# A second queue for half of the expert weights: w_up's odd expert issued from GpSimd, the rest from the sync engine

## The chip, the cores and the metric

One core of a Trainium2 chip. The metric is the device time of one execution of the whole kernel, in microseconds. All tensors are float32, batch 1, 256 tokens.

## The reference

A decoder block of width 1024: a mixer (causal pooling beside sliding-window attention, merged by sigmoid gates), then a mixture of experts with 32 experts of which each token uses 4. What costs the time is the second part:

```python
def moe(h, w_router, b_router, w_up, b_up, w_down, b_down):
    logits = (t @ w_router + b_router).astype(jnp.float32)
    top_vals, top_idx = lax.top_k(logits, TOP_K)          # TOP_K = 4
    ...
    for e in range(N_EXPERTS):                            # 32
        act = clamped_swiglu(t @ w_up[e] + b_up[e])       # w_up[e]   1024 x 2048
        out = out + gates[:, e:e + 1] * (act @ w_down[e] + b_down[e])   # w_down[e] 1024 x 1024
    return out.astype(h.dtype).reshape(B, S, D)
```

Every expert is used by some token, so all of w_up (268.4 MB) and w_down (134.2 MB) must come from HBM.

## The kernel before

**Passes and loads.** The experts are worked off in pairs, one pair to a pass, 16 passes: up to 64 tokens of the even expert lie in columns 0 to 63 of the gathered activations, those of the odd expert in columns 64 to 127. A pass takes 12 loads of 2 MiB: 8 of w_up (`UP_LOADS`; four column chunks `j` times two halves of the contraction) and 4 of w_down. Each load fills one slot of `ring`, which has `R` = 10 slots. In a w_up slot the first half holds the even expert's 1 MiB and the second half the odd expert's; each of these comes by a DMA of its own with rows of 2 KiB (`load_expert`, L274 to L284). A w_down load has rows of 8 KiB; the last one of a pass is cut in two with rows of 4 KiB (L289, L292, L293).

**Who issues.** All these DMAs are issued by the sync engine (SP) in one order: `load` 0 to 11 of one pass after the other, the first pass at L317 to L323, the others in a hardware loop of 3 rounds of 5 passes (L335 to L340). Ahead of each load SP waits until TensorE has freed the slot. Since there are 10 slots and 12 loads, `wait_freed` (L325) makes load n of a pass wait for load n + 2 of the pass before (for n below 10), counted in `up_done` and `down_done`. Each slot has a semaphore `full[slot]` that rises by `LANDED` = 32 when the whole slot has landed (16 for each of the two halves of w_up).

**The mixer** is ordered by a list of units (`UNITS`, counted in `unit_done`). Its eleven loads use the same ring; the ones that matter here are the last four (`C_GA`, `C_GA2`, `W_OUT0`, `W_OUT1`), which SP issues after the unit attn1, and after them the first pass's loads, each of which waits for the unit that used its slot last.

**TensorE.** `pe_pass` does a pass: for each chunk a bias matmul (L747) and two loads of matmuls (L768, 8 a load), transposes of the activation (L739), then the four w_down loads (L789, 16 a load), the gather for the next pass (L721), the scatter (L806) and a transpose (L730). `slot_load` (L818) waits for `full` of the slot. VectorE and ScalarE do the activation between them.

**GpSimd** sets some constants at the start, adds up the pooling windows, and issues two DMAs of the mixer (`skew` L390 and `band` L405); after about 46 us it has nothing to do.

Of the kernel before, what the change touches and what calls it, by code (L numbers as in the profile page):

```python
# [15 lines left out]
P = 128  # L16
# [19 lines left out]
PASSES = E // 2  # L36
ROUNDS = SEQ // SLOTS - 1
LISTED = 16
NJ, CH = 4, 512
# [4 lines left out]
R = 10  # L44
SLOT = KD * CH
LANDED = 32

C_U, C_KV, C_Q, C_GP, W_POOL, C_GPA, W_ATTN, C_GA, C_GA2, W_OUT0, W_OUT1 = range(11)
MIXER_LOADS = 11
# [4 lines left out]
LOADS = 12  # L54
UP_LOADS = 2 * NJ
UNROLL = 5
# [15 lines left out]
UNIT = {name: n for n, (name, _) in enumerate(UNITS)}  # L72
# [22 lines left out]
def hybrid_block_kernel(nc, x, norm1_g, w_in, pool_w, pool_scale, w_pool_proj, sinks, w_attn_proj,  # L95
# [4 lines left out]
    w_in_d, w_up_d, w_down_d = w_in[0], w_up[0], w_down[0]  # L100
# [6 lines left out]
    with ExitStack() as ctx:  # L107
        def sb(name, shape, dt=F32):
            return ctx.enter_context(nc.sbuf_tensor(name, shape, dt))

        def sem(name):
            return ctx.enter_context(nc.semaphore(name))

        ring = sb("ring", [P, R, SLOT])
# [94 lines left out]


        full = [sem(f"slot{i}_full") for i in range(R)]
        x_loaded = [sem("x0_loaded"), sem("x1_loaded")]
        vec_loaded, bias_in_loaded = sem("vec_loaded"), sem("bias_in_loaded")
        pw_loaded, sinks_loaded, router_loaded = sem("pw_loaded"), sem("sinks_loaded"), sem("router_loaded")
# [3 lines left out]
        unit_done = sem("unit_done")  # L218
# [12 lines left out]
        up_done = sem("up_done")  # L231
# [4 lines left out]
        down_done = sem("down_done")  # L236
# [11 lines left out]
        def emptied_at(name):  # L248

            n = UNIT[name]  # L250
            by = UNITS[n][1]
            return emptied[by], sum(b == by for _, b in UNITS[:n + 1])
# [10 lines left out]
        @block.sync  # L263
        def _(sp):
            def load_w_in(n, c):
                wide = min(CH, w_in_d.shape[1] - c * CH)
                sp.dma_start(ring[:, n % R, 0:KD * wide].rearrange("p (k n) -> p k n", k=KD),
                             w_in_d[:, c * CH:c * CH + wide].rearrange("(k p) n -> p k n", p=P)).then_inc(full[n % R], LANDED)

            def load_rows(n, src):  # L270
                sp.dma_start(ring[:, n % R, :].rearrange("p (k n) -> p k n", n=D),
                             src.rearrange("(k p) n -> p k n", p=P)).then_inc(full[n % R], LANDED)

            def load_expert(slot, load, expert):  # L274


                dst = ring[:, slot, :]
                if load < UP_LOADS:
                    cols, half = slice(load // 2 * CH, (load // 2 + 1) * CH), slice(load % 2 * CH, (load % 2 + 1) * CH)
                    for e in range(2):  # L280
                        src = w_up_d[bass.ds(expert + e, 1), half, cols].rearrange("e (k p) n -> p (e k) n", p=P)
                        sp.dma_start(dst[:, e * SLOT // 2:(e + 1) * SLOT // 2].rearrange("p (k n) -> p k n", n=CH),  # L282
                                     src).then_inc(full[slot], LANDED // 2)
                else:  # L284
                    m = load - UP_LOADS
                    src = w_down_d[bass.ds(expert, 2), m * CF:(m + 1) * CF, :].rearrange("e (p k) n -> p e (k n)", p=P)
                    dst = dst.rearrange("p (e n) -> p e n", e=2)
                    if load < LOADS - 1:
                        sp.dma_start(dst, src).then_inc(full[slot], LANDED)  # L289
                    else:  # L290

                        sp.dma_start(dst[:, :, 0:D], src[:, :, 0:D]).then_inc(even_landed, 16)  # L292
                        sp.dma_start(dst[:, :, D:2 * D], src[:, :, D:2 * D]).then_inc(full[slot], LANDED)  # L293

            for t in range(TT):
                sp.dma_start(acc[:, t, :], x_d[t]).then_inc(x_loaded[t], 16)

            sp.dma_start(vectors[0:KD, :], norm1_g[0].rearrange("(k p) -> k p", p=P)).then_inc(vec_loaded, 16)
            sp.dma_start(vectors[KD:2 * KD, :], norm2_g[0].rearrange("(k p) -> k p", p=P)).then_inc(vec_loaded, 16)
            sp.dma_start(vectors[2 * KD:2 * KD + KW, :], pool_scale[0].rearrange("(k p) -> k p", p=P)).then_inc(vec_loaded, 16)  # L300
            for n in (C_U, C_KV, C_Q, C_GP):
                load_w_in(n, W_IN_LOAD.index(n))
            load_rows(W_POOL, w_pool_proj[0])
            load_w_in(C_GPA, W_IN_LOAD.index(C_GPA))
            load_rows(W_ATTN, w_attn_proj[0])

            sp.wait_ge(unit_done, UNIT["pool1"] + 1)
            sp.dma_start(bup, b_up_d).then_inc(bup_loaded, 16)

            sp.wait_ge(unit_done, UNIT["attn1"] + 1)  # L310
            load_w_in(C_GA, W_IN_LOAD.index(C_GA))
            load_w_in(C_GA2, W_IN_LOAD.index(C_GA2))
            load_rows(W_OUT0, w_out[0][0:CH, :])
            load_rows(W_OUT1, w_out[0][CH:D, :])

            last_use = ["gate_pool1", "q1", "gate_pool5", "gate_pool7", "gate_attn1", "gate_attn7",
                        "gate_attn5", "gate_attn7", "out3", "out3"]  # L317
            for load in range(LOADS):
                if load < R:
                    sp.wait_ge(unit_done, UNIT[last_use[load]] + 1)  # L320
                else:
                    sp.wait_ge(up_done, load - R + 1)
                load_expert((MIXER_LOADS + load) % R, load, 0)  # L323

            def wait_freed(g, load):  # L325

                back, g0 = load - R, 0
                if back < 0:
                    back, g0 = back + LOADS, -1
                if back < UP_LOADS:  # L330
                    sp.wait_ge(up_done, UP_LOADS * (g + g0) + (back + 1))
                else:
                    sp.wait_ge(down_done, 4 * (g + g0) + (back - UP_LOADS + 1))

            with sp.Fori(0, (PASSES - 1) // UNROLL) as i:  # L335
                for q in range(UNROLL):
                    g = i * UNROLL + (q + 1)
                    for load in range(LOADS):
                        wait_freed(g, load)
                        load_expert((MIXER_LOADS + (q + 1) * LOADS + load) % R, load, g * 2)  # L340


            sp.wait_ge(extra_ready, 1)
            extras = sp.value_load(n_extra[0:1, 0:1], min_val=0, max_val=LISTED)
            with sp.If(extras > 0):
                with sp.Fori(0, extras) as t:
                    pair = sp.value_load(x_pair[0:1, bass.ds(t, 1)], min_val=0, max_val=PASSES - 1)
                    for load in range(LOADS):
                        if load < R:

                            sp.wait_ge(down_done, (t + PASSES) * 4)
                        else:
                            sp.wait_ge(up_done, (t + PASSES) * UP_LOADS + (load - R + 1))
                        load_expert((ALL_LOADS + load - LOADS) % R, load, pair * 2)
            with sp.Else():
                pass

            sp.wait_ge(up_done, (extras + PASSES) * UP_LOADS - (UP_LOADS - 3))
            sp.dma_start(fin_g, final_g.partition_broadcast(P)).then_inc(fin_loaded, 16)
            sp.wait_ge(result_ready, 1)  # L360
            sp.dma_start(out_d[0], result[:, 0, :]).then_inc(stored, 16)
            for n in range(2):
                sp.wait_ge(result_ready, n + 2)
                sp.dma_start(out_d[1][:, n * CH:(n + 1) * CH], result[:, 1, n * CH:(n + 1) * CH]).then_inc(stored, 16)
            sp.wait_ge(stored, 16 * 3)
# [3 lines left out]
        def _(pool):  # L369
# [19 lines left out]
            src = bias_row.unsqueeze(1).broadcast_to([HEADS, P, 3 * WINDOW])  # L389
            nc.gpsimd.dma_start(skew.rearrange("p h i -> h p i"), src).then_inc(skew_written, 16)  # L390

            src = uT
            for step in range(NG):
# [7 lines left out]
                src = dst  # L401
            pool.wait_ge(skew_written, 16)
            pitch = HEADS * 3 * WINDOW
            back = bass.AP(skew.tensor, WINDOW - 1, [[pitch - 1, P], [3 * WINDOW, HEADS], [1, 2 * WINDOW]])
            nc.gpsimd.dma_start(band, back).then_inc(band_loaded, 16)  # L405


        @block.scalar
# [124 lines left out]
        def _(pe):  # L533
# [94 lines left out]
            for i in range(6):  # L628
# [3 lines left out]
                for n in range(4):  # L632
                    if i < 4:
                        src = scores1[:, 2 * i + n // 2, (n % 2) * P:(n % 2 + 1) * P]
                    else:
                        src = scores0[:, 4 * (i - 4) + n, :]
# [179 lines left out]
            def main_slot(i, q):  # L816

                def slot_load(load):  # L818
                    n = MIXER_LOADS + q * LOADS + load
                    pe.wait_ge(full[n % R], i * (LANDED * UNROLL * LOADS // R) + LANDED * (n // R + 1))  # L820
                    return ring[:, n % R, :]
                return slot_load

# [339 lines left out]
```

## Time and profile before

| | |
|---|---|
| median of the runs | 1203.43 us (3 runs, 1203.12 to 1203.86) |
| the profiled execution, span from the first to the last instruction | 1200.5 us |
| TensorE busy | 1105.0 us, 92% |
| VectorE, ScalarE, GpSimd busy | 249.1, 101.6 and 8.9 us |
| moved by DMA | 431.72 MB, 360 GB/s over the span |

The profile shows one execution, whose span is some 3 us shorter than the median of the times, which include what lies around it. The rows further down give busy time by stretch, what the queues moved and what was waited for. The share of a DMA queue can add up to a little over 100%, since the records of packets that follow each other overlap by a few ns.

### The profile page before, as it was taken

The numbers are of one execution on the slowest core, as the hardware profiler recorded it, in microseconds if no ns is written. First come the engines' busy times: TensorE is split into PE (matmuls) and PEld (weight loads), VectorE is DVE, ScalarE is ACT, GpSimd is POOL, SyncE is SP. The second block draws the span as 40 slices with busy tenths as digits, with TensorE's granted clock in tenths as the row PEclk, the third lists the DMA queues.
The fourth block names the chain that finished last, engine by engine and source line by source line (L and its number), as shares of the span: only waits on it lengthen the run. The fifth ranks groups of instructions, "written<-read, shape, count | busy, mean of one in ns | idle before, by whom it ended". The sixth has DMA issues, their size and how long they took to land.

```text
span 1200.5 us, 12804 instructions
## 1 busy us (share of the span) xinstructions
PE 1105.0 (92%) x4941; PEld 498.7 (42%) x4941; DVE 249.1 (21%) x567; ACT 101.6 (8%) x257; POOL 8.9 (1%) x20
## 2 busy tenths in 40 slices
PE   6599998999999999899998989988998989898986
PEld 4488865333434343334342423333333424243332
DVE  2132114121221212122211212111121212121122
ACT  1041012000000000000000000000000000000002
POOL 0200000000000000000000000000000000000000
PEclk9799997999999999899999999998999999999999
DMA  8740995899999999999999999999999999999995
GB/s 240 242 155 2 366 387 196 302 387 407 387 407 387 408 387 407 387 403 390 401 394 397 397 392 403 389 405 386 405 385 407 387 407 385 406 389 401 393 397 208
DMA packets 170500, 431.72 MB, mean 360 GB/s; under 512 B 7479, under 2 KB 9196, under 8 KB 158148
## 3 DMA queue, kind: packets, MB, share of 16 engines
q1 hardware_dynamic: 167368, 427.59, 93.7%
q0 software_dynamic: 976, 2.63, 1.3%
q8 instruction: 47, 0.77, 0.3%
q10 hardware_dynamic: 2092, 0.60, 0.2%
q14 instruction: 17, 0.14, 0.0%
HBM read 428.16 MB, written 2.62 MB: 359 GB/s over the span
## 4 chain that ended last, share of the span: by engine, by line
SPq 64%; PE 24%; DMA 5%; issue 4%; DVE 1%; ACT 0%; DVEq 0%; ACTq 0%
SPq L282 56%; PE bank L564 9%; PE bank L768 6%; SPq L289 5%; DMA ring<-in_w_in 4%; PE bank L789 3%; PE bank L667 2%; DMA ring<-in_w_down 2%; SPq L293 1%; SPq L292 1%; PE bank L721 1%; PE bank L747 1%; PE bank L806 0%; PE bank L684 0%; PE bank L581 0%
## 5 line engine op out<-in xcount | busy, mean ns | idle before, releaser
L768 PE MATMUL bank<-ring,z_buf 128*64 128x512 f32 x2048 | 463.4, 602 | 28.7 <-DMA ring<-in_w_up 28.5
L768 PEld LDWEIGHTS bank<-ring,z_buf 128*64 128x64 f32 x2048 | 141.8, 138 | 345.1 <-issue 279.0
L789 PE MATMUL bank<-ring,m_buf 128*64 128x512 f32 x1024 | 228.3, 596 | 11.5 <-DMA ring<-in_w_down 11.3
L789 PEld LDWEIGHTS bank<-ring,m_buf 128*64 128x64 f32 x1024 | 75.2, 137 | 144.3 <-issue 130.9
L1059 DVE TENSOR_SCALAR swi<-bank 128x256 f32<-128x256 f32 x64 | 27.2, 425 | 390.3 <-PE bank L768 390.3
L564 PE MATMUL bank<-h_buf,ring 128*128 128x256 f32 x400 | 91.9, 386 | 15.4 <-DMA ring<-in_w_in 14.4
L564 PEld LDWEIGHTS bank<-h_buf,ring 128*128 128x128 f32 x400 | 76.9, 194 | 26.9 <-DMA ring<-in_w_in 14.8
L747 PE MATMUL bank<-pw_buf,row_buf 128*128 128x512 f32 x128 | 69.9, 629 | 16.9 <-issue 10.3
L498 ACT ACTIVATE swi<-swi 128x256 f32<-128x256 f32 x64 | 26.7, 416 | 586.2 <-DVE swi L1059 586.2
L721 PEld LDWEIGHTS bank<-u_buf,h_buf 128*128 128x128 f32 x512 | 61.2, 196 | 25.3 <-issue 25.3
L721 PE MATMUL bank<-u_buf,h_buf 128*128 128x128 f32 x512 | 67.4, 286 | 0.1
L806 PE MATMUL bank<-y,u_buf 128*128 128x512 f32 x128 | 61.9, 606 | 1.0
L1070 DVE COPY y<-bank 128x512 f32<-128x512 f32 x16 | 11.1, 692 | 239.7 <-PE bank L789 239.7
L1044 DVE TENSOR_TENSOR z_buf<-bank,small 128x512 f32<-128x512 f32 x32 | 22.1, 692 | 143.0 <-PE bank L721 143.0
L1049 DVE TENSOR_TENSOR acc<-acc,bank 128x512 f32<-128x512 f32 x64 | 43.9, 686 | 11.6 <-PE bank L806 11.1
L739 PEld LDWEIGHTS bank<-ident,m_buf 128*128 128x128 f32 x128 | 20.1, 206 | 52.3 <-issue 52.3
L492 ACT COPY m_buf<-bank 128x256 f32<-128x256 f32 x64 | 23.0, 359 | 142.2 <-PE bank L739 142.2
L806 PEld LDWEIGHTS bank<-y,u_buf 128*128 128x128 f32 x128 | 21.6, 189 | 30.5 <-DVE acc L1049 21.0
L739 PE MATMUL bank<-ident,m_buf 128*128 128x128 f32 x128 | 32.3, 334 | 0.0
L777 PE MATMUL bank<-rt_buf,row_buf 128*128 128x256 f32 x128 | 30.3, 379 | 0.0
L667 PE MATMUL bank<-ring,m_buf 128*128 128x512 f32 x64 | 29.5, 621 | 0.0
L747 PEld LDWEIGHTS bank<-pw_buf,row_buf 128*128 128x128 f32 x128 | 20.2, 199 | 20.8 <-issue 10.8
(163 smaller groups left out, 380.7 us busy)
## 6 DMA issues: line engine op xcount, KB each, us to landing
ring<-in_w_up SPq DMA_DIRECT2D x256, 1024.0 KB
ring<-in_w_down SPq DMA_DIRECT2D x48, 2048.0 KB
ring<-in_w_down SPq DMA_DIRECT2D x32, 1024.0 KB, 23.4
ring<-in_w_in SPq DMA_DIRECT2D x6, 2048.0 KB
ring<-in_w_out SPq DMA_DIRECT2D x2, 2048.0 KB
ring<-in_w_pool_proj SPq DMA_DIRECT2D x1, 2048.0 KB
ring<-in_w_attn_proj SPq DMA_DIRECT2D x1, 2048.0 KB
skew<-y POOLq DMA_DIRECT2D x1, 1536.0 KB, 35.2
```

What stands on the lines that cost most here:

```text
L282: sp.dma_start(dst[:, e * SLOT // 2:(e + 1) * SLOT // 2].rearrange("p (k n) -> p k n", n=CH), src).then_inc(full[slot], LANDED // 2)
L289: sp.dma_start(dst, src).then_inc(full[slot], LANDED)
L564: ins = nc.tensor.matmul(dst, w[:, k, c * P:(c + 1) * P], rhs[:, k, :], start=(k == 0), stop=(k == kn - 1))
L667: ins = nc.tensor.matmul(b[:, :], mixedT[:, k, t * P:(t + 1) * P], w[:, k % 4, n * CH:(n + 1) * CH], start=(k == 0), stop=(k == KD - 1))
L721: ins = nc.tensor.matmul(turn_banks[k // 4][:, (k % 4) * P:(k % 4 + 1) * P], x1r[:, t, k * P:(k + 1) * P], pick[:, t, :], start=(t == 0), ...
L739: ins = nc.tensor.transpose(turn_banks[j % 2][:, c * P:(c + 1) * P], hid[:, j * CF + c:(j + 1) * CF:2], ident[:, :])
L747: nc.tensor.matmul(up_banks[j % 2][:, :], rows[:, j].rearrange("p e s -> p (e s)"), bup, start=True, stop=False, skip_group_check=True)
L768: ins = nc.tensor.matmul(b[e * SLOTS:(e + 1) * SLOTS, :], xgT[:, at, e * SLOTS:(e + 1) * SLOTS], w[:, e, k, :], start=False, stop=(at == K ...
L777: nc.tensor.matmul(down_banks[n][:, c * CF:(c + 1) * CF], rows[:, 2 * n + c].rearrange("p e s -> p (e s)"), bdn, start=(c == 0), stop=Fals ...
L789: ins = nc.tensor.matmul(down_banks[n][e * SLOTS:(e + 1) * SLOTS, :], hidT[:, k, e * SLOTS:(e + 1) * SLOTS], w[:, e, k % 2, n * CH:(n + 1) ...
L806: nc.tensor.matmul(scatter_banks[q % 2][:, :], spreadT[:, t * P:(t + 1) * P], y[:, n * CH:(n + 1) * CH], start=True, stop=True).then_inc(s ...
L1049: nc.vector.tensor_tensor(acc[:, t, n * CH:(n + 1) * CH], acc[:, t, n * CH:(n + 1) * CH], scatter_banks[q % 2][:, :], ALU.add).then_inc(ad ...
```

## The change

A second set of ten semaphores, `odd_full`, is added. In the main passes SP issues only the even expert's half of each w_up slot and lets `full[slot]` rise by 32 with it; w_down stays with SP as it was. The odd expert's half is issued by GpSimd in a loop of its own, with the same conditions on the slot. TensorE waits for both semaphores ahead of a w_up load. The branch for extra passes (more than 64 tokens for an expert) still loads both halves from SP; it isn't taken with these inputs.

```diff
+        odd_full = [sem(f"slot{i}_odd_full") for i in range(R)]
...
-            def load_expert(slot, load, expert):
+            def load_expert(slot, load, expert, experts=(0, 1)):
...
-                    for e in range(2):
+                    for e in experts:
...
-                                     src).then_inc(full[slot], LANDED // 2)
+                                     src).then_inc(full[slot], LANDED // len(experts))
...
-                load_expert((MIXER_LOADS + load) % R, load, 0)
+                load_expert((MIXER_LOADS + load) % R, load, 0, experts=(0,))
...
-                        load_expert((MIXER_LOADS + (q + 1) * LOADS + load) % R, load, g * 2)
+                        load_expert((MIXER_LOADS + (q + 1) * LOADS + load) % R, load, g * 2, experts=(0,))
...
             nc.gpsimd.dma_start(band, back).then_inc(band_loaded, 16)
+
+            def load_odd_expert(slot, load, expert):
+                cols, half = slice(load // 2 * CH, (load // 2 + 1) * CH), slice(load % 2 * CH, (load % 2 + 1) * CH)
+                src = w_up_d[bass.ds(expert + 1, 1), half, cols].rearrange("e (k p) n -> p (e k) n", p=P)
+                nc.gpsimd.dma_start(ring[:, slot, SLOT // 2:SLOT].rearrange("p (k n) -> p k n", n=CH), src).then_inc(odd_full[slot], 16)
+
+            last_use = ["gate_pool1", "q1", "gate_pool5", "gate_pool7", "gate_attn1", "gate_attn7", "gate_attn5", "gate_attn7"]
+            for load in range(UP_LOADS):
+                pool.wait_ge(unit_done, UNIT[last_use[load]] + 1)
+                load_odd_expert((MIXER_LOADS + load) % R, load, 0)
+            with pool.Fori(0, (PASSES - 1) // UNROLL) as i:
+                for q in range(UNROLL):
+                    g = i * UNROLL + (q + 1)
+                    for load in range(UP_LOADS):
+                        back = load - R + LOADS
+                        if back < UP_LOADS:
+                            pool.wait_ge(up_done, UP_LOADS * (g - 1) + (back + 1))
+                        else:
+                            pool.wait_ge(down_done, 4 * (g - 1) + (back - UP_LOADS + 1))
+                        load_odd_expert((MIXER_LOADS + (q + 1) * LOADS + load) % R, load, g * 2)
...
                     pe.wait_ge(full[n % R], i * (LANDED * UNROLL * LOADS // R) + LANDED * (n // R + 1))
+                    if load < UP_LOADS:
+                        nth = sum(m % LOADS < UP_LOADS and (MIXER_LOADS + m) % R == n % R for m in range(q * LOADS + load + 1))
+                        pe.wait_ge(odd_full[n % R], i * (16 * UNROLL * UP_LOADS // R) + 16 * nth)
```

## Rows read from the trace of the kernel before

**Rows 1.** Windows: busy us of each engine, clock, DMA share and rate.
```profile
222.00:1181.00 959.00, 901.69 (x4006) 347.52 (x4002) 189.65 (x417) 59.08 (x157) 0.00 (x0) 0.99 1.04 396
84.00:120.00 36.00, 36.00 (x215) 31.96 (x213) 9.63 (x16) 8.51 (x23) 0.00 (x0) 1.00 0.01 1
267.00:324.00 57.00, 56.48 (x257) 22.02 (x258) 12.32 (x27) 3.78 (x10) 0.00 (x0) 1.00 1.04 398
1068.00:1131.00 63.00, 57.06 (x257) 22.36 (x256) 12.32 (x27) 3.78 (x10) 0.00 (x0) 1.00 1.04 397
```

**Rows 2.** The page: shares of the chain of work that ended last.
```profile
SPq 64%; PE 24%; DMA 5%; issue 4%; DVE 1%; ACT 0%; DVEq 0%; ACTq 0%
```

**Rows 3.** The DMA view, 142 to 160 us, all w_up: packets, MB, share.
```profile
DMA packets 3512, 6.97 MB, mean 387 GB/s; under 512 B 111, under 2 KB 111, under 8 KB 3512
q1 hardware_dynamic: 3512, 6.97, 105.2%
```

**Rows 4.** The DMA view, 1163 to 1173 us, mostly w_down.
```profile
DMA packets 620, 4.21 MB, mean 421 GB/s; under 512 B 32, under 2 KB 32, under 8 KB 131
```

**Rows 5.** SP's instructions in order: start, us, line, count.
```profile
126.18 48.28 SPq L282 DMA_DIRECT2D ring<-in_w_up  x16
194.95 18.35 SPq L289 DMA_DIRECT2D ring<-in_w_down  x3
219.33 0.37 SPq L292 DMA_DIRECT2D ring<-in_w_down  x1
222.94 1.12 SPq L282 DMA_DIRECT2D ring<-in_w_up  x2
```

**Rows 6.** GpSimd's last DMA in order, and the page's row with its landing.
```profile
45.07 0.92 POOL L405 DMA_DIRECT2D ring<-skew  x1 [7.81 <-DMA skew<-y]
ring<-skew POOLq DMA_DIRECT2D x1, 1024.0 KB, 9.8
```

**Rows 7.** The DMA view, 50 to 52 us: both queues at work (q0 is GpSimd's).
```profile
DMA packets 206, 0.72 MB, mean 358 GB/s; under 512 B 1, under 2 KB 1, under 8 KB 206
q0 software_dynamic: 145, 0.59, 82.9%
q1 hardware_dynamic: 61, 0.12, 18.0%
```

**Rows 8.** The DMA view, 128 to 131 us: rows of 1 KiB on SP's queue.
```profile
DMA packets 881, 1.09 MB, mean 362 GB/s; under 512 B 16, under 2 KB 816, under 8 KB 881
```

**Rows 9.** The DMA view, 132 to 140 us: rows of 4 KiB on SP's queue.
```profile
DMA packets 815, 3.27 MB, mean 409 GB/s; under 512 B 16, under 2 KB 16, under 8 KB 815
```

**Rows 10.** TensorE's instructions in order, the mixer's gates.
```profile
125.44 3.62 PE L564 MATMUL bank<-h_buf,ring 128*128 128x256 f32 x16
128.90 1.89 PE L564 MATMUL bank<-z_buf,ring 128*128 128x256 f32 x8
130.62 3.62 PE L564 MATMUL bank<-h_buf,ring 128*128 128x256 f32 x16
```

**Rows 11.** TensorE in order, pass 1: its first up matmuls and last down ones.
```profile
266.90 1.51 PE L768 MATMUL bank<-ring,z_buf 128*64 128x512 f32 x6
310.03 7.09 PE L789 MATMUL bank<-ring,m_buf 128*64 128x512 f32 x32
```

**Rows 12.** TensorE in order, the end of pass 14 and pass 15.
```profile
1117.26 7.09 PE L789 MATMUL bank<-ring,m_buf 128*64 128x512 f32 x32 [0.91 <-DMA ring<-in_w_down]
1131.84 3.65 PE L768 MATMUL bank<-ring,z_buf 128*64 128x512 f32 x16
1181.16 7.09 PE L789 MATMUL bank<-ring,m_buf 128*64 128x512 f32 x32 [0.88 <-DMA ring<-in_w_down]
1188.18 1.98 PE L806 MATMUL bank<-y,u_buf 128*128 128x512 f32 x4
```

**Rows 13.** The chain of waits, the last load of all: start, us.
```profile
1157.72 0.05 issue
...
1157.91 23.11 DMA ring<-in_w_down
```

**Rows 14.** TensorE's waits for w_up, from 222 to 640 us, then to 1181 us: total, times, longest.
```profile
PE bank L768 <- DMA ring<-in_w_up: 0.2, 1, 0.2
...
PE bank L768 <- DMA ring<-in_w_up: 28.5, 25, 2.2
```

## The prediction, made before the change was run

> **What bounds the kernel now.** I read the windows first, because a busy share over the whole span mixes stages. From 222 us to 1181 us, 959 of the span's 1200.5 us, the DMA engines are busy without a break (share 1.04) and move 396 GB/s [rows 1]. TensorE is at work 902 of these 959 us, which looks like a second limit; the single passes settle it. Pass 1, which finds its data in place, takes TensorE 57 us with 56.5 busy; pass 14 takes 63 us with 57.1 busy [rows 1]. The 6 us are waits for data. The chain of waits says the same by the queue: 64% of the span is SP in the act of issuing [rows 2], that is, SP held up by a DMA queue that is full. The rate checks too: in a stretch of w_up alone the engines move 387 GB/s [rows 3], in one that is nearly all w_down 421 GB/s [rows 4]. A pass has 16.78 MB of w_up and 8.39 MB of w_down: 43.4 + 19.9 = 63.3 us, the length of a late pass. So the end is set by bytes over rate, counted from the moment when the stream last stood still, and by what TensorE still has to do once the last byte is there.
>
> That moment is 222.9 us. SP had issued the first pass's w_up by 174.5 us and then waited until 194.95, 219.33 and 222.94 us for slots that TensorE had to free [rows 5].
>
> **Part 1: early loads in the mixer.** GpSimd can issue the first odd halves as soon as their slots are free, ahead of attn1. Between 84 and 120 us the DMA engines do nothing (1 GB/s) [rows 1], so up to 4 MiB can land there for nothing. I cost this at 0. The stream stands still again until 222.9 us for want of slots [rows 5], and the ring holds no more than before; what was fetched earlier only lengthens that pause. There could be a small loss: `C_GA` is issued at 120.3 us and needed by the third gate_attn unit at 130.6 us [rows 10]. If one odd half (1.05 MB, 2.7 us at 387 GB/s) passes it, it lands about 130 instead of 127 us. Nought to 2.7 us; I take 0.
>
> **Part 2: issue time.** SP issues 128 DMAs fewer, but it spends its time waiting for a full queue, not working. 0. TensorE gets 128 more semaphore waits, in the DMA-bound passes inside its idle 6 us; only the last pass could show its eight of them. The short steps of issue in the chain are 0.05 us each [rows 13]; 0 to 0.4 us, I take 0.
>
> **Part 3: the rate of the two queues together.** Nothing here shows a w_up load on GpSimd's queue. The nearest rows are its one load into the ring, with rows of 1 KiB: while it runs, both queues together move 358 GB/s, in packets of 4 KiB (0.59 MB in 145) [rows 7]. SP's queue with rows of the same 1 KiB moves 362 GB/s in a stretch that holds a few larger packets too [rows 8]. For equal rows the two queues are worth the same, so I take 387 GB/s for the odd halves as well: 0. The bounds: if the packing into 4 KiB packets makes 2 KiB rows as good as SP's 4 KiB rows, 409 GB/s [rows 9], the 8.39 MB of odd halves in a pass take 20.5 in place of 21.7 us, 1.2 us by 15 passes, -18 us. If any mixture of the queues runs at 358 GB/s, it covers the odd halves and a fifth as much again of SP's (0.12 beside 0.59 MB [rows 7]), 10.1 MB: 28.2 us instead of 25.8 at the 391 that lies between rows 3 and 4, 2.4 us by 15 passes, +36 us.
>
> **Part 4: the order in which the bytes come.** This is where I see a cost. Before, one queue brings the bytes in just the order in which TensorE wants them. Now GpSimd's queue carries 8 of the 24 half-loads of a pass and its only brake is the freed slot. In the one place where the queues met, q0 moved 0.59 MB and q1 0.12 MB in 2 us [rows 7]: GpSimd's data passes SP's, and also the backlog that stands in SP's queue (the last load waits 23 us between issue and landing [rows 13]). GpSimd's load took 9.8 us from issue to landing, with 1024 rows [rows 6]; one of 512 rows, at most every 7.9 us, can be kept up. So the odd halves will be as far ahead as the ring allows, and the bytes that they take early are missing in SP's stream, on which TensorE then waits. In the middle this costs nothing, as the engines are always busy. At the end it does. The odd halves of pass 15 need slots that pass 14 frees, the last two after its second w_down load. All eight are there, or nearly, when the last w_down load of pass 14 lands. Behind that landing stand only SP's own bytes of pass 15: 8.39 MB at 387 and 8.39 MB at 421 GB/s, 21.7 + 19.9 = 41.6 us. The last byte still lands at 1181.2 us (parts 1 and 3), so pass 14's last w_down lands at 1139.6 instead of 1117.3 us [rows 12]. From there TensorE is the bound: 14.6 us to the first up matmul of pass 15 (1117.26 to 1131.84 [rows 12]), 50.2 us from that to the last down matmul when no data is late (266.90 to 317.12 in pass 1 [rows 11]), 12.3 us from there to the end (1188.25 to 1200.5 [rows 12]). 1139.6 + 14.6 + 50.2 + 12.3 = 1216.7 us, against 1200.5 now. In other words, after the last byte TensorE has 23 us of matmuls left and not 7.
>
> **The sum.** 0 + 0 + 0 + 16.2 us on a span of 1200.5 us. The median is 2.9 us above the profiled span, which I leave: 1219.6 us.
>
> **The Trainium skill on this.** Its page DMA: Bandwidth & Descriptors, section "Issuing engines are not separate DMA queues", says that DMAs from several engines run on the same 16 DMA engines and interleave, so that a second issuer only saves issue time. It speaks against any gain here. By that rule alone the time would stay as it is, at 1203.4 us; it agrees with rows 7 and 8 as to the rate and says nothing of part 4.
>
> **Rivals.** *A, the forecast*: order costs 16 us, the rate is within a per cent or so. *B, faster*: the odd halves go at up to 409 GB/s and the lead is smaller than I think, because with 2 KiB rows the queues share evenly. With no lead at all that is 1203.4 - 18 = 1185.4 us; with the whole lead 1201.6 us. For it speaks the size of q0's packets; against it the 358 GB/s of rows 7. It decides for faster where the rate gains more than the order costs, at 5% on the odd halves with the whole lead. *C, no change*: the engines serve both queues so that the halves of a slot come together, and the rate is the same: 1203.4 us. For it, the same bytes and engines; against it, 145 packets beside 61. *D, much slower*: the mixture is slow, 1219.6 + 36 = 1256 us, or GpSimd can't write its descriptors fast enough. If each of its loads took the 9.8 us of rows 6 with none overlapping, a pass would need 78 us and the kernel some 225 us more. Rows 6 are for twice as many rows, so I hold that for improbable. *E, the change does not do what it says*: the odd halves wait on the same slots so late that GpSimd gains no lead; its time is that of C.
>
> **How the numbers follow.** A 0.73, between 1206 and 1250 us (part 3 taken from a small gain to most of the loss); B 0.12, from 1185 to 1202; C and E 0.09, about 1203; D 0.06, above 1250. A measurement of this kernel tells 0.2% (2.4 us) from no change. Slower by more than that: 0.73 + 0.06 = 0.79. Within it: 0.09. Faster: 0.12. The range from 1203 to 1250 us holds A and the upper part of C, 0.79 together. The likeliest time is A's, 1219.6 us.
>
> **What the profile will show.** Rate: in a middle pass the DMA share stays at about 1.04 and the rate near 396 GB/s; 380 or less means the mixture is slow, 403 or more that B is right. Order: TensorE's waits for data begin passes earlier (up to 640 us they are 0.2 us now, behind it 28.5 [rows 14]), and these are for SP's halves; in the last pass there are none, the last w_down lands near 1181 us, and the last down matmul ends near 1204 us, over 20 us behind it. If instead the last w_down matmuls start with their data, as now, part 4 is wrong. If GpSimd's issues lie further apart than 8 us with its slots free, it is D. What would make the forecast wrong above all is the rate, on which 959 us depend: each per cent of it is worth 9.6 us.

## The result, and the profile after

The changed kernel takes 1207.41 us (median of 4 runs, 1205.68 to 1209.60), the kernel before beside it 1203.28 us: a ratio of 1.0054 with a 95% interval from 1.0031 to 1.0077. A second measurement, on the same chip as three of the experiments below, gave 1.0062 (1.0041 to 1.0084). The ratios here and below are those on record, which aren't the quotients of the medians printed beside them: these two medians lie 4.1 us apart, and a ratio of 1.0054 is 6.5 us. So the kernel is slower, by some 4 to 7 us, in the direction forecast; the forecast of 16 us was more than double.

The profiled execution is the slowest of the four, 1209.6 us, with a span of 1207.6 us against 1200.5 before. First the page: both queues, the chain, and the new instructions. It answers to rows 2 (there SP 64%, TensorE 24%).

```profile
q1 hardware_dynamic: 99784, 293.36, 63.5%
q0 software_dynamic: 35792, 136.85, 30.2%
...
PE 46%; SPq 29%; DMA 20%; issue 2%; DVE 1%; ACT 1%; DVEq 0%; ACTq 0%
...
L412 POOL DMA_DIRECT2D ring<-in_w_up x128 | 96.1, 751 | 987.5 <-PE bank L790 577.3
...
ring<-in_w_up POOLq DMA_DIRECT2D x128, 1024.0 KB, 17.3
```

GpSimd's 128 issues take 0.75 us each and wait for TensorE, that is for slots; descriptors are no bottleneck. TensorE, not SP, is now the largest part of the chain that ended last. The rate is untouched: the long window that stood in rows 1 reads the same here, 396 GB/s at a share of 1.03.

```profile
222.00:1181.00 959.00, 903.58 (x3978) 348.05 (x3974) 189.90 (x418) 58.68 (x156) 90.16 (x120) 0.98 1.03 396
```

So the 7 us of the spans are not in the rate of the stream. TensorE in order, pass 14's end and pass 15, which answers to rows 12:

```profile
1129.09 5.37 PE L811 MATMUL bank<-ring,m_buf 128*64 128x512 f32 x24
1135.96 1.94 PE L811 MATMUL bank<-ring,m_buf 128*64 128x512 f32 x8 [1.50 <-DMA ring<-in_w_down]
...
1145.38 3.65 PE L790 MATMUL bank<-ring,z_buf 128*64 128x512 f32 x16
...
1181.05 7.09 PE L811 MATMUL bank<-ring,m_buf 128*64 128x512 f32 x32
...
1188.50 7.09 PE L811 MATMUL bank<-ring,m_buf 128*64 128x512 f32 x32
```

To compare the end of pass 14 with the kernel before, one must know which load the waits are for. Each w_down load makes 16 of the matmuls that the profile counts, so the 32 that begin at 1117.26 and at 1181.16 us in rows 12 belong to the third and the last w_down load of a pass, and the wait in front of them is for the third. Rows 13 agree: what was issued at 1157.91 us and landed 23.1 us later is the last of the three DMAs of L289, not the last load of all. The last load's second half held up TensorE's weight loads a little, later on. From the kernel before, passes 14 and 15:

```profile
1122.29 0.32 PEld L789 LDWEIGHTS bank<-ring,m_buf 128*64 128x64 f32 x4 [0.54 <-DMA ring<-in_w_down]
...
1186.06 0.45 PEld L789 LDWEIGHTS bank<-ring,m_buf 128*64 128x64 f32 x4 [0.41 <-DMA ring<-in_w_down]
```

The reader should see two things. The second half of pass 14's last w_down load, the last data of that pass, is there at 1136.0 us, against 1122.3 before: in the changed kernel the wait stands before the last 8 matmuls and is for that half. And from 1145.4 us on no row has a wait for data: pass 15 runs from its first up matmul to its last down one in 50.2 us, just the length of pass 1 in rows 11, and ends at 1195.6 against 1188.2 us. The 7.3 us between these two are the difference of the spans but for 0.2.

The granted clock is not the reason. Over the whole execution its mean is 0.968, against 0.980 before, but in this last stretch it is 1.00, the upper of its levels (2.4 GHz):

```profile
1145.00:1196.00 51.00, 51.00 (x233) 18.70 (x232) 7.48 (x18) 3.68 (x10) 0.00 (x0) 1.00 0.79 309
```

The waits that TensorE lost time in, up to 640 us and from there to 1190 us, answer to rows 14:

```profile
PE bank L811 <- DMA ring<-in_w_down: 11.1, 4, 3.3
...
PE bank L811 <- DMA ring<-in_w_down: 25.8, 11, 3.6
```

They begin earlier, as forecast, and all of them are for w_down, whose data comes from SP alone; for w_up there are none, where before 28.5 of 39.8 us were for w_up. In total TensorE waits 36.9 us for data up to 1190 us, no more than before: what costs is where the lag stands at the end, not the sum of the waits.

### The profile page after: what moved, and what is told of

Same layout as the page of the kernel before. It is cut to its first block, busy times and chain, and to the rows that moved or that the text cites. A ratio compares the mean times of both kernels' runs of the same rounds, so it can differ in the third digit from the quotient of the medians.

```text
span 1207.6 us, 13044 instructions
## 1 busy us (share of the span) xinstructions
PE 1114.0 (92%) x4941; PEld 501.4 (42%) x4941; DVE 249.2 (21%) x567; ACT 101.6 (8%) x257; POOL 105.1 (9%) x148
## 4 chain that ended last, share of the span: by engine, by line
PE 46%; SPq 29%; DMA 20%; issue 2%; DVE 1%; ACT 1%; DVEq 0%; ACTq 0%
SPq L283 25%; PE bank L790 17%; DMA ring<-in_w_down 17%; PE bank L586 9%; PE bank L811 7%; PE bank L743 4%; DMA ring<-in_w_in 4%; SPq L290 3%; PE bank L769 3%; PE bank L689 2%; PE bank L828 2%; SPq L293 1%; PE bank L761 1%; PE bank L799 1%; DVE acc L1074 1%
## 5 line engine op out<-in xcount | busy, mean ns | idle before, releaser
L790 PE MATMUL bank<-ring,z_buf 128*64 128x512 f32 x2048 | 457.6, 599 | 1.3 <-issue 1.0
L811 PE MATMUL bank<-ring,m_buf 128*64 128x512 f32 x1024 | 241.5, 622 | 36.9 <-DMA ring<-in_w_down 36.9
L412 POOL DMA_DIRECT2D ring<-in_w_up x128 | 96.1, 751 | 987.5 <-PE bank L790 577.3
L743 PEld LDWEIGHTS bank<-u_buf,h_buf 128*128 128x128 f32 x512 | 63.2, 201 | 28.5 <-issue 28.5
## 6 DMA issues: line engine op xcount, KB each, us to landing
ring<-in_w_up POOLq DMA_DIRECT2D x128, 1024.0 KB, 17.3
```

Of the source, the lines that this page charges most:

```text
L412: nc.gpsimd.dma_start(ring[:, slot, SLOT // 2:SLOT].rearrange("p (k n) -> p k n", n=CH), src).then_inc(odd_full[slot], 16)
L743: ins = nc.tensor.matmul(turn_banks[k // 4][:, (k % 4) * P:(k % 4 + 1) * P], x1r[:, t, k * P:(k + 1) * P], pick[:, t, :], start=(t == 0), ...
L790: ins = nc.tensor.matmul(b[e * SLOTS:(e + 1) * SLOTS, :], xgT[:, at, e * SLOTS:(e + 1) * SLOTS], w[:, e, k, :], start=False, stop=(at == K ...
L811: ins = nc.tensor.matmul(down_banks[n][e * SLOTS:(e + 1) * SLOTS, :], hidT[:, k, e * SLOTS:(e + 1) * SLOTS], w[:, e, k % 2, n * CH:(n + 1) ...
```

## Experiments

Theory O says that the order costs: GpSimd's queue runs ahead, and at the end TensorE has more left than SP's stream. Its rivals are R (the rate of two queues together), W (TensorE's additional waits) and Q (the second queue as such). Ratios are to the kernel before on the same chip.

### The waits alone

```diff
-                                     src).then_inc(full[slot], LANDED // 2)
+                                     src).then_inc(*((full[slot], LANDED // 2) if not apart else (odd_full[slot], 16) if e else (full[slot], LANDED)))
...
+                        pe.wait_ge(odd_full[n % R], i * (16 * UNROLL * UP_LOADS // R) + 16 * nth)
```

> The kernel before with the second set of semaphores and TensorE's 128 more waits, but both halves issued by SP. Theory O (order: GpSimd's queue runs ahead, so that the last pass is short of SP's half and TensorE is the bound there): the time of before, 1203.3 us within 1.5. Rival W (the waits themselves cost): near the changed kernel, 1206 to 1208 us.

Measured: 1200.32 us, ratio 0.9997 (0.9982 to 1.0012). The waits cost nothing; W is out.

### The last pass from one queue

```diff
-                        load_expert((MIXER_LOADS + (q + 1) * LOADS + load) % R, load, g * 2, experts=(0,))
+                        load_expert((MIXER_LOADS + (q + 1) * LOADS + load) % R, load, g * 2,
+                                    experts=(0, 1) if last and q == UNROLL - 1 else (0,))
...
+            odd_round((PASSES - 1) // UNROLL - 1, UNROLL - 1)
```

> The changed kernel, except that both halves of the last pass (15) come from SP; GpSimd stops after pass 14. Theory O: nothing of pass 15 is taken early, the last w_down load lands some 7 us ahead of TensorE's end of the matmuls as before, and the time goes back to 1202 to 1204.5 us. Rival R (the rate of two queues together is 0.4% lower over the 959 us): only a fifteenth of the loss goes away, 1207 us. Rival W (waits): 1207 us.

Measured: 1207.78 us, ratio 1.0053 (1.0028 to 1.0077): nothing came back, and my reading of O missed; by the time alone this run speaks for R and W. Its twelve executions spread from 1199.9 to 1213.5 us, and the profiled one took 1211.9. The timeline shows what happens, TensorE at the end of pass 13 and the first up matmuls of passes 14 and 15:

```profile
1077.85 3.68 PE L818 MATMUL bank<-ring,m_buf 128*64 128x512 f32 x8 [3.48 <-DMA ring<-in_w_down]
...
1090.00 3.65 PE L797 MATMUL bank<-ring,z_buf 128*64 128x512 f32 x16
...
1147.87 3.65 PE L797 MATMUL bank<-ring,z_buf 128*64 128x512 f32 x16
...
1190.99 7.09 PE L818 MATMUL bank<-ring,m_buf 128*64 128x512 f32 x32
...
1077.80:1084.30 6.50, 6.45 (x24) 3.61 (x25) 0.69 (x1) 0.59 (x1) 0.00 (x0) 0.56 1.04 383
```

The lead is the same; it only ends a pass earlier. GpSimd's queue stops after pass 14's halves, and the wait for the second half of pass 13's last w_down load ends at 1077.9 us. From there TensorE works without a wait for data: 12.2 us to the first up matmul of pass 14, 57.9 us to that of pass 15, and 50.2 us more, with the end of the down matmuls at 1198.1 us. (In the changed kernel the first of these stretches takes 9.4 us. Here it comes behind a wait of 3.5 us, and over 6.5 us from there the granted clock is 0.56 in the mean, near the lower of its levels, 1.2 GHz.) The lag that a lead has put on TensorE is worked off only at the 5.4 us that a pass of 57.9 us gains on one of 63.3 us of bytes; a single pass can't.

### A shorter lead

```diff
-                        back = load - R + LOADS
+                        back = load - 5
+                        g0 = 0 if back >= 0 else -1
+                        back = back % LOADS
```

> The changed kernel, but GpSimd waits for each load until TensorE has finished the load 5 before it (instead of the one 10 before, which frees the slot). Two queues, same packets, shorter lead. Theory O: the odd halves run at most 5 loads ahead, little more than SP's own backlog, the last pass has nearly all its bytes in order: 1202 to 1204.5 us. Rival R: 1207 us as the changed kernel. If 5 loads are too short for the landing time of 17 us, TensorE waits for the odd halves and it is slower than 1210 us.

Measured: 1204.20 us, ratio 1.0033 (1.0017 to 1.0049), against 1.0054 and 1.0062 for the changed kernel. The time lies in the expected range and reads lower than the changed kernel's, but the intervals overlap, so the times alone don't show that a part of the loss is gone. The profile, an execution of 1203.3 us, shows more. TensorE at the end of pass 14 and of pass 15, and GpSimd's queue from 1130 to 1181 us:

```profile
1129.81 1.94 PE L815 MATMUL bank<-ring,m_buf 128*64 128x512 f32 x8 [2.13 <-DMA ring<-in_w_down]
...
1182.38 7.09 PE L815 MATMUL bank<-ring,m_buf 128*64 128x512 f32 x32
...
q0 software_dynamic: 1481, 5.67, 29.2%
```

The last down matmul ends at 1189.5 us, 1.2 us later than before, against 7.3 in the changed kernel. A balance ties this to the lead. In the kernel before, 66.0 us pass from the landing of pass 14's last half-load to the last down matmul (1122.3 to 1188.25 us), 63.8 of them until pass 15's last half-load is there. TensorE needs 59.6 us for that work when no data is late (1135.96 to 1195.59 us in the changed kernel), so it has 6.4 us of slack. Of pass 15's 8.39 MB of odd halves 5.67 MB are still to come here, so 2.72 MB came early, 7.0 us at 387 GB/s: an estimate of 0.6 us of cost, against 1.2. In the changed kernel 2.69 MB are still to come (the view is further down), so 5.70 MB came early, 14.7 us: 8.3 us, against 7.3. The estimate is good to about 1 us, and the cost goes with the lead.

### Everything from GpSimd's queue

```diff
+                    if load < LOADS - 1:
+                        nc.gpsimd.dma_start(dst, src).then_inc(odd_full[slot], LANDED)
```

(and so for w_up, both halves; the loop with its waits moved from SP to GpSimd, with semaphores of its own)

> All expert loads, w_up and w_down, from GpSimd's queue in the old order; SP issues only the mixer's. One queue, no lead of one half. Theory O: rate as SP's for w_up (387 GB/s); for w_down packets are at most 4 KiB on this queue and the rate may be 409 instead of 421 GB/s, 0.6 us a pass: between 1203 and 1213 us. Rival R (descriptors written by GpSimd make the engines slower): w_up below 380 GB/s in the windows, 1220 us or more.

Measured: 1202.46 us, ratio 1.0018 (1.0004 to 1.0031), just under the range given. The DMA view from 1128 to 1140 us, all w_up, on GpSimd's queue alone:

```profile
DMA packets 1207, 4.64 MB, mean 387 GB/s; under 512 B 74, under 2 KB 74, under 8 KB 1207
q0 software_dynamic: 1207, 4.64, 102.6%
```

387 GB/s, as in rows 3 from SP's queue. With 2 KiB rows GpSimd's queue carries two rows to a packet and is just as fast. For w_down I had expected packets of 4 KiB at most, which was wrong: from 1155 to 1175 us, while w_down comes, 655 of the 1437 packets are of 8 KiB or more, and the rate is 411 GB/s. R is out as to the queue by itself.

### The order alone, in one queue

```diff
+            for n in range(LOADS, PASSES * LOADS):
+                g, load = divmod(n, LOADS)
+                order.append((n, 0, g, load, 0))
+                if load < UP_LOADS:
+                    order.append((n - (6 if g >= 8 else 0), 1, g, load, 1))
+            for _, _, g, load, e in sorted(order):
+                wait_freed(g, load)
```

> One queue only (SP, GpSimd issues nothing of w_up), with the separate semaphores of the first experiment, but from pass 8 on SP issues the odd half of a w_up load 6 loads ahead of its place in the order (its own instructions written out, no loop). Theory O, order alone costs: when pass 14's last w_down load lands, 5 odd halves (5.24 MB, 13.5 us at 387 GB/s) of pass 15 are already there, 63.3 - 13.5 = 49.8 us of bytes stand behind it; TensorE needs 64.8 us from there to its last down matmul, against 49.8 + 7.1 = 56.9: 7.9 us slower than the control with 0 ahead, 1209 to 1213 us. Rival Q, the second queue or GpSimd's descriptors cost: no difference from the control, 1201 to 1204 us.

The control, with 0 in place of the 6:

> The control of the run before: the same kernel with SP's instructions written out, odd halves in their old place. Both theories: the time of before, within 1.5 us; if the written-out program itself costs, it shows here.

Measured: the control 1198.73 us, ratio 0.9987 (0.9973 to 1.0001); with 6 ahead 1212.26 us, ratio 1.0100 (1.0075 to 1.0125), 13.5 us above the control. GpSimd has no part in it, and the picture is that of the changed kernel. TensorE around the end of pass 14, with 6 ahead:

```profile
1139.01 1.94 PE L803 MATMUL bank<-ring,m_buf 128*64 128x512 f32 x8 [0.63 <-DMA ring<-in_w_down]
...
1148.42 3.65 PE L782 MATMUL bank<-ring,z_buf 128*64 128x512 f32 x16
...
1191.54 7.09 PE L803 MATMUL bank<-ring,m_buf 128*64 128x512 f32 x32
```

and in the control, where data is waited for to the end:

```profile
1116.65 7.09 PE L803 MATMUL bank<-ring,m_buf 128*64 128x512 f32 x32 [0.89 <-DMA ring<-in_w_down]
...
1180.03 7.09 PE L803 MATMUL bank<-ring,m_buf 128*64 128x512 f32 x32 [0.89 <-DMA ring<-in_w_down]
```

It cost more than the 7.9 us expected. A part is in the stream: with 6 ahead SP must wait for slots 4 loads behind its own place, and from 600 us on it waits 184 us for TensorE, against 66 in the control. From 640 to 1131 us the two kernels read (6 ahead, then the control)

```profile
640.00:1131.00 491.00, 440.39 (x1904) 168.30 (x1902) 90.15 (x199) 28.17 (x75) 0.00 (x0) 0.97 1.02 390
...
640.00:1131.00 491.00, 446.91 (x1978) 178.17 (x1974) 94.58 (x207) 29.10 (x77) 0.00 (x0) 0.99 1.04 396
```

and from 1175 to 1195 us the one still moves 5.24 MB, the other 3.55, of which 0.45 are already the output: 2.1 MB more, 5.3 us at 400 GB/s. In these two profiles the last down matmuls end at 1198.6 and 1187.1 us, 11.5 us apart. So 6.2 us remain for the order, near the 7.9 expected, and near the 7.1 that the balance under the shorter lead gives for 5.24 MB (13.5 us less 6.4).

### TensorE made short, both kernels

```diff
-                        for k in range(4):
+                        for k in (3,):
```

(of the four steps `k` of each up load only the last is left, so that three quarters of the up matmuls are left out and the output is not the reference's)

> The changed kernel with only every fourth up matmul of each expert load (three of four steps of the contraction over w_up left out, so its output is not the reference's); all loads as they were. TensorE needs some 21 us less in a pass and is never the bound at the end. Theory O: 14.6 + 29 = 44 us of TensorE stand behind the last w_down of pass 14 against at least 41.6 + 7.1 us of bytes and last matmuls, so the order costs nothing and the time is that of the lite kernel before within 1.5 us. Rival R (the rate of the queues together is lower): some 4 us slower than the lite kernel before.

> The kernel before with the same matmuls left out (three of four steps of the contraction over w_up): the base of the run before. Both theories: DMA-bound from the first pass on, the stream stands still less at the start since slots are freed sooner: 1180 to 1200 us.

Measured: 1195.63 us (0.9952, 0.9935 to 0.9969) and 1196.53 us (0.9968, 0.9954 to 0.9983). With TensorE no longer near the bound the change costs nothing that can be told from none. That is against R in the two-queue form, since the bytes, the packets and the two queues are those of the full kernels. In the changed kernel's short form the chain ends as in the old one, with the landing of w_down's third load and the 7 us of matmuls on the last two loads:

```profile
1152.11 22.50 DMA ring<-in_w_down
1174.75 7.09 PE bank L811 x32
```

### Both weights halved between the queues

```diff
-                    src = w_down_d[bass.ds(expert, 2), m * CF:(m + 1) * CF, :].rearrange("e (p k) n -> p e (k n)", p=P)
+                    many = len(experts)
+                    src = w_down_d[bass.ds(expert, many), m * CF:(m + 1) * CF, :].rearrange("e (p k) n -> p e (k n)", p=P)
```

(and the odd half of each w_down load in GpSimd's loop)

> As the changed kernel, but GpSimd also issues the odd expert's half of every w_down load, so both queues carry the same bytes in the same order, each held only by the freed slots. Theory O: GpSimd's queue still moves packets of 4 and 8 KiB against SP's 2 and 8 KiB, so it still runs ahead, up to 9 half-loads of 1 MiB in the ring when pass 14's last w_down lands, less the 2 to 3 that are in flight: 16 to 18 us of bytes, against about 14 in the changed kernel: 7 to 12 us above the kernel before, at least as slow as the changed one. Rival B (equal halves keep step, the unequal load of the queues was the fault): within 2 us of the kernel before.

Measured: 1211.25 us, ratio 1.0094 (1.0071 to 1.0116). Equal halves don't keep step: of the halves of the last w_down load, cut in two, GpSimd's take 8.1 us from issue to landing and SP's 24.8 (medians). The loss is there, as O has it; the ratio reads higher than the changed kernel's 1.0062, but the intervals overlap. TensorE's waits, from 222 us on, are now for w_up: 

```profile
PE bank L809 <- DMA ring<-in_w_up: 39.2, 19, 4.2
```

### Only the first pass from GpSimd

```diff
-                        load_expert((MIXER_LOADS + (q + 1) * LOADS + load) % R, load, g * 2, experts=(0,))
+                        load_expert((MIXER_LOADS + (q + 1) * LOADS + load) % R, load, g * 2)
```

(and GpSimd's loop left out; TensorE waits for `odd_full` in the first pass alone)

> GpSimd issues the odd halves of the first pass alone (in the mixer, where the DMA engines stand still); all later loads are SP's in the old order, one semaphore. Theory O: no lead at the end, and the early bytes only lengthen the pause before 222.9 us: the time of before within 1.5 us. Rival E (early loads delay the mixer's own): 1 to 3 us slower; if the early bytes were worth something, up to 10 us faster.

Measured: 1199.84 us, ratio 0.9987 (0.9975 to 1.0000). The early loads in the mixer neither cost nor bring anything that can be told from none.

### A lead of 3 loads

```diff
-                        back = load - R + LOADS
+                        back = load - 3
```

(and the rest as with 5)

> The changed kernel with GpSimd held until TensorE has finished the load 3 before its own. Theory O: the lead is no more than SP's backlog, so nothing is lost to the order; but 3 loads are some 16 us, near the 17 us that its loads took to land, so TensorE may wait for odd halves instead: between 1201 and 1206 us, with waits for w_up in the trace. Rival R (rate): 1.005 times the kernel before, whatever the lead.

Measured: 1280.42 us, ratio 1.0664 (1.0642 to 1.0686), far above the range I gave. TensorE's waits and the rate from 222 us on:

```profile
222.00:1181.00 959.00, 855.27 (x3692) 330.89 (x3690) 175.70 (x386) 54.19 (x144) 83.86 (x112) 0.97 0.98 374
...
PE bank L794 <- DMA ring<-in_w_up: 90.5, 62, 3.9
...
ring<-in_w_up POOLq DMA_DIRECT2D x128, 1024.0 KB, 12.4
```

Its waits for w_up are 62, in place of none. GpSimd's loads take 12.4 us to land, and TensorE does three w_up loads in some 12 us (in the timeline of the changed kernel's pass 15 the chunks of two begin 8.3 us apart). TensorE then waits for an odd half, 90.5 us in all, and the stream falls from 396 to 374 GB/s; that it does so because these waits hold back the slots is my reading, which no run tested. I had counted 16 us for three loads, the pace of the stream, where the pace of TensorE in the up phase counts.

### The changed kernel again

> The changed kernel itself beside the others, for a ratio from the same chip: 1.004 to 1.007 of the kernel before.

Measured: 1209.03 us, ratio 1.0062 (1.0041 to 1.0084).

## Why the prediction was right or wrong

**Part 1, early loads: 0.** Right; the first-pass experiment gave 0.9987.

**Part 2, issue and waits: 0.** Right; 0.9997.

**Part 3, the rate: 0.** Right. The long window stayed at 396 GB/s, the short forms of both kernels are 0.9 us apart, and GpSimd's queue alone moves w_up at 387 GB/s. Neither bound came near.

**Part 4, the order.** The mechanism is the one forecast, and it is shown without the second queue by the one-queue experiment. Its size was wrong: the last down matmuls end at 1195.6 us, not 1204.3. The step that failed is "All eight are there, or nearly, when the last w_down load of pass 14 lands", the size of the lead in the sum.

*The lead.* The eight odd halves of pass 15 had not landed. The DMA view of the changed kernel from 1136 to 1150 us, in which GpSimd's bytes end some way ahead of 1150:

```profile
q1 hardware_dynamic: 1366, 2.72, 53.4%
q0 software_dynamic: 709, 2.69, 50.3%
```

2.69 of GpSimd's 8.39 MB were still to come, 7.0 us at 387 GB/s, and stood behind the landing beside SP's bytes. Why so much was missing: GpSimd issued the last of these halves at 1129.4 us, and its loads take 17.3 us to land (median), not the 9.8 of rows 6. That fits how the queues share. In rows 7 I read 145 packets of q0 beside 61 of q1 and took it that GpSimd's data simply passes SP's. In steady state the packets alternate one for one. The DMA view at 600 to 603 us (SP sends w_down) and 621 to 627 us (SP sends w_up):

```profile
q1 hardware_dynamic: 103, 0.80, 65.9%
q0 software_dynamic: 102, 0.42, 34.9%
...
q0 software_dynamic: 396, 1.54, 67.0%
q1 hardware_dynamic: 392, 0.78, 36.1%
```

102 beside 103, 396 beside 392. GpSimd's packets are 4 KiB, SP's are one row: 8 KiB for w_down, 2 KiB for w_up. So GpSimd gets two thirds of the bytes while SP loads w_up and one third while it loads w_down. Here the trace agrees with the Trainium skill, page DMA: Bandwidth & Descriptors, section "Queues, rings and completion order", by which an engine alternates between its queues at packet boundaries. The page's typical packet of 9 to 17 descriptors is not what these records show, which hold one or two rows. Two microseconds of one load in a mixer were a poor row for a steady state; why the packets stood 145 to 61 there, no run shows.

*Which landing the sum speaks of.* 1117.3 and 1181.2 us in the sum, and 1157.91 plus 23.11 in rows 13, are landings of the third w_down load of a pass, not of the last byte: 1.20 MB were moved after 1180 us in the kernel before. The sum used the third load at both ends, with the 32 matmuls (7.1 us) of the last two loads behind it, so this error alone doesn't shift its result. Put for the second half of the last load, which is what TensorE waited for in the changed kernel, the sum reads 1186.1 - 41.6 = 1144.5 us, then 9.4 us from there to the first up matmul of pass 15, taken from the changed kernel, and the 50.2: 1204.1 us, nearly the same. The landing was measured at 1136.0 us. So the excess lies in the landing alone, 8.5 us: 7.0 are the bytes still to come, and 1.5 I can't split. (The stream also ended a little later: after 1180 us 1.64 MB were left, against 1.20, some 1.1 us, by which the part not accounted for grows to about 2.6.) But "after the last byte TensorE has 23 us of matmuls left and not 7" was wrong on both sides: before, the last half-load had 2.2 us behind it (1186.1 to 1188.25), and by the sum it would have had 18 (1186.1 to 1204.3).

**The rivals.** B fell on the rate, D on GpSimd's 0.75 us an issue. C and E said that no lead forms; the waits for w_down show that it does. What the profile was to show came out for the rate, for the earlier waits, and for the last pass without a wait, but not for the end of the last down matmul.

**What stays open.** The changed kernel's ratio is 1.005 to 1.006; its profile shows 7 us, the medians 4 to 7. With a lead of 5 the profile shows 1.2 us at the last down matmul and the median 3.1 us, so whether more than the order costs there isn't settled. No kernel here with the full output beats the kernel before by more than the measurement tells.

## What to carry to other kernels

If the DMA engines are full, a second queue brings no bandwidth, but it takes away the order: in this kernel the data of the queue that is held back only by free buffers arrived early, and what was needed next arrived late. Ask what compute is left when the last byte lands, and how much of the last bytes then belongs to one queue; a lead of n bytes costs n over the rate, less the slack that compute has in the passes left to catch up (here 6.4 us). A throttle on the early queue must leave its whole landing time at the pace of the consumer: 5 loads of lead cost 0.3%, 3 loads cost 6.6%.

## What the runs showed of the hardware that I had not expected

Two queues that both had work shared the engines by packets, one for one (102 beside 103, 396 beside 392), and a packet of GpSimd's queue holds two rows of 2 KiB where SP's holds one. Which queue is favoured thus changed with the row length: GpSimd's bytes to SP's were two to one beside w_up and one to two beside w_down.

The engines don't seem to finish together. In the control of the one-queue experiment SP has issued all weights by 1162 us, and the rate falls to half some 6 us ahead of the end of the weights, where each slice is 0.5 us from 1175 us on:

```profile
GB/s 434 385 426 401 442 401 393 434 369 377 254 221 221 205 213 205 180 164 156 164 131 25 0 0 0 0 0 0 0 0 0 0 0 33 0 0 0 66 401 401
```

It fits that the third w_down load lands there only at 1180.0 us, when little more than 1 MB of the weights is left, though 2.1 MB were issued behind it. The views don't tell which engines lag, and no run here tried to even them out.
